# Second recurrence of a two-block network on Trainium2: the fourth-power product of the triangular inverse as four 32 by 32 tile products per block

## What is computed

```
def step(S, inp):
    rt, vt, wt, kt, at, bt = inp
    sa = jnp.einsum('bhij,bhj->bhi', S, at)
    S = S * wt[:, :, None, :] + sa[..., None] * bt[:, :, None, :] + vt[..., None] * kt[:, :, None, :]
    return S, jnp.einsum('bhij,bhj->bhi', S, rt)
```

## Time and profile before

| | us |
|---|---|
| median of 3 runs | 3356.42 |
| the runs | 3347.96 to 3361.47 |
| the profiled execution | 3349.04 |
| its span in the trace | 3347.3 |
| PE busy in the span | 3258.2 (97%) |
| DVE busy | 2143.0 (64%) |
| ACT busy | 1548.4 (46%) |
| mean granted clock of TensorE | 0.994 of full speed |

### The profile page before, as it was taken

One profiled execution on the slowest core, in us unless ns is written; L12 is line 12 of the kernel. 1 busy time (PEld: TensorE's weight loads), 2 busy tenths in 40 slices (PEclk: granted clock), 3 DMA queues, 4 the chain that ended last, 5 costly groups with the idle time before them and its releaser, 6 DMA issues.

```text
span 3347.3 us, 82761 instructions
## 1 busy us (share of the span) xinstructions
PE 3258.2 (97%) x37068; PEld 2960.6 (88%) x37068; DVE 2143.0 (64%) x3294; ACT 1548.4 (46%) x2366; POOL 175.0 (5%) x254
## 2 busy tenths in 40 slices
PE   7999999999899999999999999999999999999988
PEld 7989999899778888888888888988899999999987
DVE  8655755567668888876655544345666766657565
ACT  5433443445444444444434444333555565556433
POOL 0000000000000000000001000001211111111010
PEclk9999999999999999999999999999999999999999
DMA  5655654765455555555554343435443343334364
GB/s 203 233 169 173 219 210 173 288 248 197 153 180 179 191 192 191 190 207 185 189 176 140 111 145 125 151 112 171 162 132 133 129 138 128 132 125 136 130 230 151
DMA packets 99713, 571.20 MB, mean 171 GB/s; under 512 B 19856, under 2 KB 26288, under 8 KB 37408
## 3 DMA queue, kind: packets, MB, share of 16 engines
q1 hardware_dynamic: 85872, 511.85, 44.3%
q0 software_dynamic: 13488, 54.06, 4.8%
HBM read 535.59 MB, written 30.28 MB: 169 GB/s over the span
## 4 chain that ended last, share of the span: by engine, by line
PE 86%; DVE 6%; issue 3%; ACT 3%; DMA 1%; POOL 0%; DVEq 0%; SPq 0%; ACTq 0%; POOLq 0%
PE banks L300 15%; PE banks L301 8%; PE banks L1069 4%; PE banks L2209 4%; PE banks L1070 4%; PE banks L1071 4%; PE banks L2210 3%; PE banks L2211 3%; PE banks L324 3%; PE banks L325 3%; PE banks L326 3%; PE banks L2431 3%; PE banks L287 3%; PE banks L288 3%; PE banks L289 3%
## 5 line engine op out<-in xcount | busy, mean ns | idle before, releaser
L267 DVE TENSOR_TENSOR w_lo<-ring,w_hi 128x2048 fp32r<-128x2048 f32 x274 | 630.6, 2301 | 427.2 <-ACT w_hi L261 427.2
L261 ACT CAST w_hi<-ring 128x2048 fp32r<-128x2048 f32 x274 | 522.7, 1908 | 225.7 <-PE banks L301 95.8
L300 PE MATMUL banks<-x_two,w_hi 128*128 128x512 f32 x1408 | 489.9, 395 | 0.0
L301 PE MATMUL banks<-x_two,w_lo 128*128 128x256 f32 x1408 | 390.8, 278 | 0.0
L1069 PE MATMUL banks<-x_two,w_hi 128*128 128x256 f32 x1152 | 342.4, 297 | 4.3 <-DVE w_lo L1143 2.4
L1070 PE MATMUL banks<-x_two,w_hi 128*128 128x256 f32 x1152 | 326.1, 283 | 0.1
L1071 PE MATMUL banks<-x_two,w_lo 128*128 128x256 f32 x1152 | 325.9, 283 | 0.0
L300 PEld LDWEIGHTS banks<-x_two,w_hi 128*128 128x128 f32 x1408 | 264.8, 188 | 61.6
L2209 PE MATMUL banks<-XK,w_hi 128*128 128x256 f32 x1024 | 304.0, 297 | 0.6 <-DVE w_lo L2265 0.5
L2210 PE MATMUL banks<-XK,w_hi 128*128 128x256 f32 x1024 | 289.6, 283 | 0.6 <-issue 0.6
L2211 PE MATMUL banks<-XK,w_lo 128*128 128x256 f32 x1024 | 289.1, 282 | 0.0
(11 more groups left out here) (573 smaller groups left out, 7706.3 us busy)
## 6 DMA issues: line engine op xcount, KB each, us to landing
ring<-in_w_up SPq DMA_DIRECT2D x88, 1024.0 KB, 4.8
ring<-in_w_dil SPq DMA_DIRECT2D x72, 1024.0 KB, 5.1
mod_ring<-in_w_mod SPq DMA_DIRECT2D x48, 1024.0 KB, 6.7
ring<-in_w_logit SPq DMA_DIRECT2D x48, 1024.0 KB, 5.2
ring<-in_w_down SPq DMA_DIRECT2D x44, 1024.0 KB, 4.8
ring<-in_w_delta SPq DMA_DIRECT2D x32, 1024.0 KB, 4.8
ring<-in_w_out SPq DMA_DIRECT2D x32, 1024.0 KB, 4.8
ring<-in_w_na SPq DMA_DIRECT2D x32, 1024.0 KB, 4.8
```

The costliest lines, as they stand in the source:

```text
L261: nc.scalar.copy(w_hi[:, s, 0:w], ring[:, s, 0:w]).then_inc(S("panel_hi"), 4)
L267: nc.vector.tensor_tensor(w_lo[:, s, 0:w], ring[:, s, 0:w], w_hi[:, s, 0:w].bitcast(F32), ALU.subtract).then_inc(S("panel_split"), 4)
L300: nc.tensor.matmul(out_ap, hi, both, start=first_, stop=False)
L301: return nc.tensor.matmul(out_ap[:, 0, :], lo, both[:, 0, :], start=False, stop=last_)
```

## The change

`s3` computes the same values from smaller pieces. For every matrix (m, c), the diagonal blocks e = 0 and 1 of `iT` (32 by 32) are multiplied with the rows of `iX` that belong to them, and the 64 columns of `iX` are taken as two halves f = 0 and 1. The wait ahead of it, the semaphore behind it, the bank and the readers stay as they are. One product of 64 rows, 64 array columns and 64 streamed columns becomes four of 32 rows, 32 array columns and 32 streamed columns. Loops run m, c, e, f from the outside in, so that two products in a row use the same 32 by 32 tile of the array, with the same weights, which are loaded for each.

```
                 pe.wait_ge(S("rw_dve"), vv("a4", b))
                 for m in range(8):
                     for c in range(2):
-                        last = nc.tensor.matmul(b8(4)[rows(c), m, :], iT[rows(c), m, :], iX[rows(c), m, :], start=True, stop=True)
+                        for e in range(2):
+                            for f in range(2):
+                                r, k = slice(64 * c + 32 * e, 64 * c + 32 * e + 32), slice(32 * f, 32 * f + 32)
+                                last = nc.tensor.matmul(b8(4)[r, m, k], iT[r, m, 32 * e:32 * e + 32], iX[r, m, k],
+                                                        start=True, stop=True)
                 last.then_inc(S("rw_mm"), 1)
                 mm.here("s3", b)
```

## The result

The changed kernel takes **3379.33 us** (median of 5 runs, 3375.59 to 3384.49) against 3352.11 (median of 5, 3347.96 to 3361.47) for the kernel before on the same chip: ratio **1.0072, interval 1.0054 to 1.0090**. It is slower by 0.7%, about 24 us. That lies inside the range given (3352 to 3384), but the point, +7.1 us, was too low by some 17 us, and the likeliest case, a change within 0.5%, was not what came. By the prediction's own two signs it is wrong: the median moved by over 17 us, and the stage from the first to the last `s3` grew by 25.4 us, not by 3 to 12.

The account below looks back on a forecast made before the run. The prediction took PE's own instruction list, busy for 97% of the span, to bound the kernel. Body +2.3 us and lost overlap +4.8 us gave +7.1 us on 3356.42, so 3363.5 us, range 3352 to 3384.

Parts of the forecast that it names:

- the prediction's own two signs: Forecast wrong if median moves over 17 us, or first-to-last s3 stage grows less than 3 or more than 12 us.
- the likeliest case: Whole kernel: measured time changes by less than 0.5% (16.8 us) either way; chance 0.77.
- The bound: Fill stage with second recurrence: PE's own list sets the end; idle time swallows at most about 1%; DVE has slack.
- Term 2: Start of s3: PE empties before the new array division, losing overlap with with_state; 0.32 us in 15 blocks, +4.8 us.
- Term 1: Body of s3: 32 turns of 31.7 ns a tile plus staggered tiles, +0.14 us a block, +2.3 us in all.
- stagger: In s3, four records in a row per tile make the last tile run up to 3 turns behind: +0.09 us a block.
- Instructions and queues: PE's list: 192 more instructions a block, 3072 in all; no DMA data transfer, semaphore or other queue changes; no time added.
- PE's waits should stay as short as now: Sign for the stage in the changed trace: PE's waits do not grow, while DVE's wait for s3 grows some 0.4 us a block.
- A: Body of s3: a 32-column turn still costs 58 ns; +17.8 us, with the lost overlap +22.6 us, 3379; chance 0.04.
- B: Inside s3: instruction supply limited to 7.3 ns each; +12.3 us, with the rest +19.4 us, 3376; chance 0.11.
- C: In s3: matmuls start strictly in order, no look past a busy tile; +39 us with lost overlap, 3395; chance 0.09.
- D: In s3: no emptying between divisions and no fixed part per turn, so nothing or a gain; -1 to +2 us; chance 0.07.

Follow-up runs that it names:

- e_turns: The changed kernel with the tile index innermost in s3 (f outside c and e), same 64 products a block; 1.0071 of the kernel before.
- e_halves: The kernel before with each 64 by 64 product of s3 issued as two halves of 32 streamed columns; 1.0061 of the kernel before.
- e_diag: The changed kernel with only the products f = e, 32 a block, leaving out those whose result is zero; 1.0010 of the kernel before.
- e_wide: The changed kernel with all 64 columns streamed per 32 by 32 tile, no halves f, 32 products a block; 1.0034 of the kernel before.
- e_after_less: The changed kernel without half of level_a, 192 PE instructions a block fewer, result not the reference's; 1.0017 of the kernel before.
- e_wa_late: The changed kernel with wa moved behind the panel products of slot D, same instructions; 1.0080 of the kernel before.

## Why the prediction was right in part and wrong in sum

**The bound: right.** PE's own list sets the end. DVE's waits for `s3` grew from 24.4 to 34.0 us, in one block more, and no wait of PE for `iX` came of it.

**Term 2, the overlap: right.** 0.17 and 0.15 us were expected, -0.169 and 0.149 measured, 4.8 us in all. The Trainium skill, "TensorEngine Tiling (Array Packing)", Key Properties, says that a change of mode drains TensorE. The starts agree with it: in each of the 15 blocks the last L2452 starts 0.148 to 0.149 us before the first L2561. The lengths of the rows don't show it, though the prediction said so: L2452's row ends at 2656.18 and L2561's begins at 2656.10, and in the earlier trace rows L2211's row ends at 2642.39 where L2452's begins at 2642.32. What the trace shows is that the starts no longer interleave.

**Term 1, the body: right in kind, its size off.** +2.3 us was reckoned, +5.0 measured (16 x 0.31: the body 0.34 longer, the step to L2407 0.03 shorter). The turn on one tile is 33 to 34 ns where 31.7 was expected, and over 31 turns that is some 0.06 us a block more: e_turns has a body of 1.096 us where 1.01 was reckoned for 32 turns. The other missed piece is the **stagger**: not 3 turns once a block (0.09 us) but 0.17 us, by e_turns, 0.08 more. With the 0.14 reckoned that gives 0.28 of the 0.31 us. Matmuls came every 1269 / 127 = 10 ns, not 8.

**The step that failed is "Instructions and queues".** It counted the 3072 instructions right and costed them at nothing, with the sentence that no other queue changes. The page of the profile has a queue for them: 292 transfers before, 304 after. Nor did the sum have a term for where ends of transfers fall. Pauses at such ends were +12.3 us (10.9 between the two repetitions), more than both terms together; "PE's waits should stay as short as now" was wrong by the same. That the result still lies in the range is luck: its upper end, 3384, was set for rivals A and B, and neither mechanism came as described. The four pauses of the earlier trace rows named "issue" were the sign. They were read as idle time that could swallow something; they were a cost that any change to the list makes anew.

**Rivals.** A is refuted by the turn of 33 to 34 ns, though its time, 3379, is the median that was measured, which is chance; e_halves shows its condition, 64 loaded columns, at 58 ns. C is refuted: late in a block four tiles start 1 to 2 ns after each other, and the better order of e_turns gains 2.8 us in the body, not 34. D is refuted by both terms. B, the instruction supply, was right in kind and wrong in place and mechanism: it priced a rate of 7.3 ns an instruction inside `s3`, and e_turns runs there at 1096 / 255 = 4.3. The supply fails at ends of transfers, mostly outside `s3`: of the waits above, 0.5 us stand at L2561, 7.0 at L2431 and 4.7 at L2407. But B was right in that a dense `s3` strains the supply: the two longest pauses of the kernel after stand in `wa` right behind it. Its price, +19.4, was near the +24 by chance.

The Trainium skill, "TensorE: Matmul & The Clock Gate", The mechanism, on strictly ordered matmuls: the trace disagrees again after the change, where late in a block four starts lie within 5 ns, 30 ns from the next four. They must be on four tiles, since one tile's turn is 33 ns, while in the program's order four records in a row are on one tile. The Trainium skill, "Runtime: NRT & Kernel Launch", Instruction fetch mechanics, says that instructions are refilled in pieces of 256 and that the cost is mostly hidden. The piece agrees with 12 transfers for 3072 instructions. "Mostly hidden" holds for the mean (6.2 us over 127 ends of pieces in the stage before, 18.6 over 139 after), not for single ones of up to 3.3 us, nor for a difference between two kernels of 0.7%.

**What stays open** is what fixes when a transfer starts. Most ends of pieces are crossed without a pause at about 5 us for 256 instructions, and many pauses stand behind pieces of that same pace; there the transfer began late, and no run here shows why. That the larger count in `s3` brings more pauses is shown by the quickly used pieces for a part, and for the sum as a tendency: 5 to 10 us in kernels with 16 products a block, 10 to 13 with 32 (e_diag, e_wide, e_halves), 15 to 20 with 64 (e_turns, e_after_less and e_wa_late among them). By how much a single rearrangement changes them can't be forecast from this. How much of the +12.3 is the count and how much the luck of the placement is bounded, not settled: the kernel before stands well (6.2 and 7.5; 10.1 shifted by half a piece), and the changed one has 18.6 and 19.6.

No version here with the reference's result beats the kernel before by a measured amount. e_diag comes closest, with 1.0010, and drops products of zeros.

## What to carry to other kernels

Where PE is busy for 97% and its list is long, count its instructions as a cost: read the queue of instruction transfers and the "issue" waits of the kernel before, and put an interval of several us on any edit that adds or moves hundreds of them; test it by moving the program by half a transfer. A split like this one leaves the streamed columns of each tile as they were, so there is nothing to win unless work is dropped with it, and it pays for the change of division (0.32 us a block here, where neighbours had interleaved before). The longest pauses (3.3 and 3.7 us) stood behind a dense run of small products that had just used up a piece of 256 instructions. Keep the tile index innermost (2.8 us here).

## What the runs showed of the hardware that was not expected

- PE pauses for 0.4 to 3.7 us at some ends of 256 instructions of its list (8 of 127 in the stage before, 15 of 139 after), mostly at the same ones in each execution of a kernel (six of eight before and 15 of 15 after recurred); a shift by 128 instructions puts them elsewhere in the program, one by 256 brings five of eight back.
- It never went past such an end sooner than 2.15 us after the start of the instruction transfer with the same running number (1839 ends in 14 traces). At one end the time for the piece ahead and the pause added up to 5.2 to 5.4 us in four traces, however fast the piece was used up.
- Without an end of a piece in the way, PE takes a weight load or a matmul every 4.3 ns over 128 pairs (e_turns), a turn of each of four 32 by 32 tiles in 33 to 34 ns.
- A turn of float32 went by the larger of its loaded and streamed columns: 58 ns for 64 and 32, 56 for 32 and 64, 33 to 34 for 32 and 32.
- The step between divisions of the array, from last start to first start, was 0.149 us from quarters to 32 by 32 tiles and 0.121 from those to halves.
